# A two-layer hybrid block on one core: the late weights' low parts in one subtraction for two halves, and the SSD norm's sums of squares on VectorE in place of POOL

## The chip, the core and the metric

The kernel runs on one core of one Trainium2 chip. The metric is device time in microseconds (us), the median of several executions. Engines: TensorE (PE; its weight loads are PEld), VectorE (DVE), ScalarE (ACT), GpSimd (POOL) and SyncE (SP), which issues the DMAs.

## The reference, cut to what matters

256 tokens of width 1024 pass through two layers (SwiGLU feed-forward, a mixer, a second feed-forward) and then through a third block with attention, a short convolution and a feed-forward. The change lies in the mixers of the two layers. A mixer projects the normed x with `w_in` and hands the result to three mixers side by side: SSD, mLSTM and RWKV-7.

```python
for l in range(DEPTH):                                        # 2 layers
    x = x + FFN_HALF * swiglu(rms_norm(x, ffn1_norm[l]), ffn1_w_gate_up[l], ffn1_w_down[l])
    u = rms_norm(x, mix_norm[l]) @ w_in[l]
    u_ssd, u_ml, u_rw = jnp.split(u, [D_SSD_IN, D_SSD_IN + D_MLSTM_IN], axis=-1)
    ...
    y = jnp.concatenate([y_ssd, y_ml, y_rw], axis=-1)
    x = x + y @ w_out[l]
    x = x + FFN_HALF * swiglu(rms_norm(x, ffn2_norm[l]), ffn2_w_gate_up[l], ffn2_w_down[l])

# the end of ssd_mixer: gate, then a norm over each of two groups of 512 channels
y = y.reshape(bsz, t, SSD_WIDTH) * jax.nn.silu(z.astype(jnp.float32))
return group_rms_norm(y, norm_g, G).astype(u.dtype)
```

## The kernel before, in words

**Split products.** Every matrix product is made of three: a weight W is split into a high part (ScalarE copies it into a tile of type fp32r) and a low part (VectorE subtracts the high part from W), and x likewise. The product is high W times high x, high W times low x and low W times high x.

**The projection.** `w_in` gives 40 tiles of 128 channels. The first 14 take weights in blocks of 128x2048 through WH and WL. The other 26, tiles 14 to 39, take the late weights. These come as 52 units of 128x512 (four k of one tile each) in the ring of weight slots, u = 0 to 51, tile 14 + u/2. For each unit ScalarE writes the high part into one of four places in the ring's third slot (`act_late_high`, L1089), VectorE subtracts in place in the first or second slot (`dve_late_low`, L1095), and TensorE does twelve matmuls (`pe_proj`, L1140 to L1142) of 256 columns. ScalarE may write high u once half u - 4 is done. The DMA of unit u + 8 waits for half u.

**What sets the order.** A mixer's work is written as strands: the projection, the scan, the RWKV and SSD strands and others, each a generator on each engine. One table of turns, the same on all engines, says in which order strands advance. Each engine executes its instructions in that order and waits on semaphores. The projection has 86 turns, two for each of i = 0 to 42. `late_at(step, ahead)` tells which unit is due at a turn: u = step + ahead - 28, for u of 4 and more. ScalarE has ahead = 3 and VectorE ahead = 2, so ScalarE makes high u + 1 in the turn in which VectorE makes low u. TensorE does half u two turns after VectorE's. In a turn i ScalarE also takes tile i from PSUM (L1191, L1192) and makes the tanh of tile i - 2 (L1181); VectorE does three taps of a convolution for tile i - 1 (L1222) and a product for tile i - 3 (L1262).

**Other strands beside it.** In the first third of a mixer ScalarE has, for RWKV, the gates (L1646), keys (L1649, L1650, L1653) and L1658, and for mLSTM the copies of q and k (L1396, L1397). VectorE has an inverse root (`dve_rsqrt`, L535 to L551) of the key norms, whose sums TensorE makes at L1609, its spreading (L1689), and the key products (L1694, L1696).

**The SSD norm.** VectorE gates Y (L2254), ScalarE squares it for each of two groups into XE, 128x1024 (L2191), POOL folds that to 128x512 and to 128x256 (L2279, L2281), TensorE sums over channels (L2148), VectorE takes the inverse root (`dve_rsqrt`) and scales (L2263). At the same time the last steps of the RWKV recurrence (L1992, L1999, L2002 on VectorE, L1773 and L1782 on TensorE, L1906 on ScalarE) and another norm's inverse root run.

Of the kernel before, what the change touches and what calls it, by code (L numbers as in the profile page):

```python
# [7 lines left out]
F32 = mybir.dt.float32  # L8
I32 = mybir.dt.int32
F32R = mybir.dt.float32r  # L10
ALU = mybir.AluOpType
# [251 lines left out]
def hybrid_kernel(nc, xin, wst, lp, sp2, cst, out):  # L263
    ctx = ExitStack()
    with ctx:
# [805 lines left out]
        def late_weights(of, l, u):  # L1071
            return of[:, late_slot(l, u % 8 // 4), 512 * (u % 4):512 * (u % 4) + 512]

        def late_high(l, u):
            return ringr[:, late_slot(l, 2), 512 * (u % 4):512 * (u % 4) + 512]

        def late_at(step, ahead):

            u = step + ahead - 4 * EARLY
            if u < 4:  # L1080
                return u // 2 + 3 if u in (-6, -4, -2, 0) else None
            return u if u < 52 else None

        def act_late_high(e, l, u):
            if u is None:
                return
            e.wait_ge(*(p_pe.on("half", l, u - 4) if u >= 4 else freed(place["w_in", l, ("two", EARLY - 1)])))
            e.wait_ge(s_late[u % 8], 16 * (u // 8 + 1 + (l * (7 if u % 8 < 4 else 6))))
            e.do.activation(late_high(l, u), late_weights(ring, l, u), ACT.Copy).then_inc(*w_act.up("late high", l, u))  # L1089

        def dve_late_low(e, l, u):
            if u is None:
                return
            e.wait_ge(*w_act.on("late high", l, u))
            e.do.tensor_tensor(late_weights(ringr, l, u), late_weights(ring, l, u), late_high(l, u).bitcast(F32), ALU.subtract).then_inc(  # L1095
                *w_dve.up("late low", l, u))

        def act_x_high(e, l, k):
# [10 lines left out]
        def pe_proj(e, l):  # L1109
            f = 2 * l  # L1110
            for i in range(43):
                n, s, b = i // 2, i % 2, tile_bank(i)
                for half in range(2):
# [11 lines left out]
                    if i < 40:  # L1125
                        for kt in range(4 * half, 4 * half + 4):
# [4 lines left out]
                                m = three(e, b[:, 0:T], turn_of("w_in", l, ("two", n)), at, XNH[:, kt, 0:T], XNL[:, kt, 0:T], kt == 0, kt == KT - 1)  # L1131
                            else:
                                u = 2 * (i - 2 * EARLY) + half
                                e.wait_ge(*w_dve.on("late low", l, u))
                                if i == 2 * EARLY:
                                    e.wait_ge(*p_act.on("xh", l, kt))
                                    e.wait_ge(*p_dve.on("xl", l, kt))
# [105 lines left out]

        def dve_proj(e, l):
            for i in range(43):
                dve_late_low(e, l, late_at(2 * i, 2))
                yield
                if split_at(i):
                    dve_low(e, turn_of("w_in", l, ("two", i // 2)) + AHEAD)
# [25 lines left out]
                if i == 13:  # L1275
                    dve_x_low(e, l, 6)
                    dve_x_low(e, l, 7)
                dve_late_low(e, l, late_at(2 * i + 1, 2))
                yield


# [801 lines left out]
        def pe_ssd(e, l):  # L2083
# [59 lines left out]
            for _ in range(3):  # L2143
                yield
            for g in range(2):
                e.wait_ge(*d_pool.on("squares", l, g))
                for c in range(2):
                    m = e.do.matmul(b[:, 2 * g + c:2 * g + c + 1], (xd, xe)[g][:, 128 * c:128 * c + 128], ones[:, 0:1], start=True, stop=True)  # L2148
            m.then_inc(*d_pe.up("sums", l))
# [51 lines left out]
        def dve_ssd(e, l):  # L2201
# [50 lines left out]
            for g in range(2):  # L2252
                yo = Y[:, 4 * g:4 * g + 4, :]
                e.do.tensor_tensor(yo, yo, XC[:, 4 * g:4 * g + 4, :], ALU.mult).then_inc(*d_dve.up("gated", l, g))  # L2254
            for _ in range(4):
                yield
            e.wait_ge(*d_pe.on("sums", l))
            dve_rsqrt(e, d_dve, b[:, 0:4], 4, 1.0 / 512, EPS, 128, ("rstd", l))
            yield
# [13 lines left out]
        def pool_ssd(e, l):  # L2273
            for _ in range(25):
                yield
            for g in range(2):
                q = (xd, xe)[g]
                e.wait_ge(*d_act.on("sq", l, g))
                e.do.tensor_tensor(q[:, 0:512], q[:, 0:512], q[:, 512:1024], ALU.add).then_inc(*d_pool.up())  # L2279
                e.wait_ge(*d_pool.last())  # L2280
                e.do.tensor_tensor(q[:, 0:256], q[:, 0:256], q[:, 256:512], ALU.add).then_inc(*d_pool.up("squares", l, g))  # L2281
            for _ in range(9):
                yield
            for k in (0, 2, 4, 6):
                pool_y_low(e, d_act, d_pool, l, k)
            yield
# [881 lines left out]
```

## Time and profile before

| | |
|---|---|
| median of 3 runs | 1691.65 us (1691.17 to 1695.12) |
| the profiled execution, its own time | 1693.02 us |
| its span | 1691.2 us |
| TensorE busy | 1644.3 us, 97% |
| VectorE busy | 1352.4 us, 80% |
| ScalarE busy | 982.1 us, 58% |
| POOL busy | 400.5 us, 24% |
| weights read from HBM | 279.53 MB |

All times inside the trace count from the start of the span. Layer 0's mixer ends at about 455 us; the late weights are used in layer 0 from 249 to 411 us and in layer 1 until 1078. The busy time of an instruction includes the end in which the next one has already begun, so the chain of waits shows a little less for each of a row of instructions than the list of instructions does. The number in brackets behind a row is the time for which the engine stood idle before it, and who ended the wait.

### The profile page before, as it was taken

To read this page: it belongs to the slowest core of one execution; us is meant where nothing else is said; L and a number is where in the kernel's file an instruction comes from. 1 tells how busy PE (TensorE), PEld (TensorE's weight loads), DVE (VectorE), ACT (ScalarE), POOL (GpSimd) and SP (SyncE) were. 2 spreads that over 40 slices of the span, in tenths; PEclk is the share of its full clock that TensorE was granted. 3 is DMA by queue.
4 is the path that set the end of the run, shared out by engine and by line. 5 is a ranking of instruction groups with operands and counts; after the bars stand their busy time and mean duration, and the time that the engine had idled before them with its cause. 6 is when DMAs were issued, how large, how long until landed. Compare 5 with 4: busy or idle time off the path is not lost.

```text
span 1691.2 us, 34343 instructions
## 1 busy us (share of the span) xinstructions
PE 1644.3 (97%) x14376; PEld 1503.0 (89%) x14376; DVE 1352.4 (80%) x2263; ACT 982.1 (58%) x1787; POOL 400.5 (24%) x312
## 2 busy tenths in 40 slices
PE   9999999998999999999999999899999999999997
PEld 7888998898898888888898989799888898999987
DVE  6887789999768886788778999876887675889974
ACT  5775448635457764676445764455774556457652
POOL 1673000000115740377100000011763100211110
PEclk9999999999899999999999999899999999999999
DMA  7765634312266655576462431135675632345442
GB/s 262 258 258 197 220 102 121 107 40 78 78 241 233 242 195 207 215 256 226 172 226 76 125 107 47 53 127 203 235 263 171 226 140 101 111 162 188 163 161 100
DMA packets 96233, 282.78 MB, mean 167 GB/s; under 512 B 7376, under 2 KB 61264, under 8 KB 73040
## 3 DMA queue, kind: packets, MB, share of 16 engines
q1 hardware_dynamic: 96080, 280.60, 47.2%
q8 instruction: 113, 1.85, 0.4%
q14 instruction: 40, 0.33, 0.1%
HBM read 279.53 MB, written 1.05 MB: 166 GB/s over the span
## 4 chain that ended last, share of the span: by engine, by line
PE 76%; DVE 19%; ACT 3%; issue 1%; DMA 1%; POOL 0%; SPq 0%; DVEq 0%; ACTq 0%
PE banks L528 29%; PE banks L529 15%; PE banks L520 8%; PE banks L521 7%; PE banks L522 7%; DVE ringr L1095 3%; DVE XC L1222 1%; DVE WL L491 1%; PE banks L1773 1%; PE banks L573 1%; DVE MS L2231 1%; PE banks L1782 1%; DVE ML L1535 1%; DMA ring<-wst 1%; PE banks L1140 1%
## 5 line engine op out<-in xcount | busy, mean ns | idle before, releaser
L491 DVE TENSOR_TENSOR WL<-ring,WH 128x2048 fp32r<-128x2048 f32 (+1 forms) x218 | 457.4, 2110 | 108.8 <-ACT WH L486 108.6
L528 PE MATMUL banks<-XNP,WH 128*128 128x512 f32 x1408 | 496.5, 397 | 3.4 <-DVE XNP L627 2.4
L486 ACT ACTIVATE WH<-ring 128x2048 fp32r<-128x2048 f32 (+1 forms) x222 | 378.9, 1715 | 52.2 <-PE banks L522 46.2
L529 PE MATMUL banks<-XNP,WL 128*128 128x256 f32 x1408 | 392.3, 279 | 0.0
L528 PEld LDWEIGHTS banks<-XNP,WH 128*128 128x128 f32 x1408 | 265.0, 188 | 65.5 <-DVE XNP L627 3.2
L990 POOL TENSOR_TENSOR HP<-G,HP 128x256 fp32r<-128x256 f32 x110 | 210.3, 1912 | 311.6 <-ACT HP L802 311.6
L528 PE MATMUL banks<-HP,WH 128*128 128x512 f32 x770 | 267.7, 392 | 0.8 <-POOL HP L990 0.7
L529 PEld LDWEIGHTS banks<-XNP,WL 128*128 128x128 f32 x1408 | 265.6, 189 | 0.0
L529 PE MATMUL banks<-HP,WL 128*128 128x256 f32 x770 | 215.2, 280 | 0.0
L528 PEld LDWEIGHTS banks<-HP,WH 128*128 128x128 f32 x770 | 144.5, 188 | 33.4 <-POOL HP L990 1.6
L520 PE MATMUL banks<-XNQ,WH 128*128 128x256 f32 (+1 forms) x544 | 157.9, 290 | 2.2 <-ACT BIG L2497 1.0
L522 PE MATMUL banks<-XNQ,WL 128*128 128x256 f32 (+1 forms) x544 | 154.8, 285 | 0.0
L521 PE MATMUL banks<-XNQ,WH 128*128 128x256 f32 (+1 forms) x544 | 154.4, 284 | 0.0
L529 PEld LDWEIGHTS banks<-HP,WL 128*128 128x128 f32 x770 | 144.6, 188 | 0.0
L1141 PE MATMUL banks<-XNr,ringr 128*128 128x256 f32 x416 | 116.4, 280 | 0.0
L900 DVE TENSOR_TENSOR G<-banks,G 128x512 f32<-128x512 f32 x88 | 60.4, 686 | 67.9 <-ACT G L896 67.6
L2279 POOL TENSOR_TENSOR XE<-XE 128x512 f32<-128x512 f32 x4 | 5.1, 1269 | 443.2 <-ACT XE L2191 443.1
L520 PEld LDWEIGHTS banks<-XNQ,WH 128*128 128x128 f32 x544 | 103.9, 191 | 6.7 <-issue 3.9
L521 PEld LDWEIGHTS banks<-XNQ,WH 128*128 128x128 f32 x544 | 104.3, 192 | 0.0
L522 PEld LDWEIGHTS banks<-XNQ,WL 128*128 128x128 f32 x544 | 104.1, 191 | 0.0
L790 POOL TENSOR_TENSOR ring<-ring 128x512 f32<-128x512 f32 x72 | 96.6, 1341 | 28.2 <-ACT ring L782 24.5
L589 POOL TENSOR_TENSOR ACC<-ACC,SQ 128x256 f32<-128x256 f32 x48 | 35.6, 741 | 260.8 <-ACT SQ L863 200.4
(538 smaller groups left out, 3786.5 us busy)
## 6 DMA issues: line engine op xcount, KB each, us to landing
ring<-wst SPq DMA_DIRECT2D x179, 1024.0 KB, 4.8
ring<-wst SPq DMA_DIRECT2D x80, 704.0 KB, 4.2
ring<-wst SPq DMA_DIRECT2D x104, 256.0 KB, 2.8
LP<-lp SPq DMA_DIRECT2D x1, 1872.0 KB, 8.4
LP<-lp SPq DMA_DIRECT2D x4, 448.0 KB, 5.5
ring<-wst SPq DMA_DIRECT2D x2, 512.0 KB, 6.1
X<-xin SPq DMA_DIRECT2D x2, 512.0 KB, 7.0
out<-X SPq DMA_DIRECT2D x4, 256.0 KB, 2.2
```

The lines of the kernel that those rows point to most:

```text
L486: e.do.activation(WH[:, slot[q], 0:n], ring[:, slot_at(i), 0:n], ACT.Copy).then_inc(*w_act.up("high", q))
L491: e.do.tensor_tensor(WL[:, slot[q], 0:n], ring[:, slot_at(i), 0:n], WH[:, slot[q], 0:n].bitcast(F32), ALU.subtract).then_inc(*w_dve.up("lo ...
L520: e.do.matmul(o, WH[:, s, cols], xh, start=first, stop=False)
L521: e.do.matmul(o, WH[:, s, cols], xl, start=False, stop=False)
L522: return e.do.matmul(o, WL[:, s, cols], xh, start=False, stop=last)
L528: e.do.matmul(b[:, :], WH[:, s, cols], x.rearrange("p s t -> p (s t)"), start=first, stop=False)
L529: return e.do.matmul(b[:, 0:T], WL[:, s, cols], x[:, 0, :], start=False, stop=last)
L790: e.do.tensor_tensor(wt[:, 0:512], wt[:, 0:512], wt[:, 512 * p:512 * p + 512], ALU.add).then_inc(*f_pool.up())
L900: e.do.tensor_tensor(G2[:, j % 3, :, :], pair_halves(j, 0), G2[:, j % 3, :, :], ALU.add).then_inc(*f_dve.up("added", f, j))
L990: e.do.tensor_tensor(HL[:, j, :], HT[:, j % 3, :], HH[:, j, :].bitcast(F32), ALU.subtract).then_inc(*f_pool.up("hl", f, j))
L1095: e.do.tensor_tensor(late_weights(ringr, l, u), late_weights(ring, l, u), late_high(l, u).bitcast(F32), ALU.subtract).then_inc(*w_dve.up(" ...
L1141: e.do.matmul(b[:, 0:T], wh, XNr[:, kt, :], start=False, stop=False)
```

## The change

VectorE makes the low parts of two units in one subtraction of 128x1024. `late_pair_at` gives the pair's even unit: pair 0 and pair 2 stand where low 1 and low 3 stood, every other pair u where low u stood; where low u + 1 stood for odd u + 1 there is nothing. The pair waits for high u + 1, and TensorE waits, for both halves, on the pair. ScalarE's, TensorE's and SyncE's instructions and their order are the same as before. In the SSD strand the two folding additions of each group go from POOL to VectorE, the first group's one turn after the gating, the second's a turn later. The number of turns of each strand stays.

```diff
+        def late_pair_at(step):
+
+            u = late_at(step, 2)
+            return u - 1 if u in (1, 3) else u if u is not None and u >= 4 else None
+
...
+        def late_tile(of, l, u):
+            return of[:, late_slot(l, u % 8 // 4), 512 * (u % 4):512 * (u % 4) + 1024]
+
         def dve_late_low(e, l, u):
-            if u is None:
+
+            if u is None or u % 2:
                 return
-            e.wait_ge(*w_act.on("late high", l, u))
-            e.do.tensor_tensor(late_weights(ringr, l, u), late_weights(ring, l, u), late_high(l, u).bitcast(F32), ALU.subtract).then_inc(
+            e.wait_ge(*w_act.on("late high", l, u + 1))
+            high = ringr[:, late_slot(l, 2), 512 * (u % 4):512 * (u % 4) + 1024]
+            e.do.tensor_tensor(late_tile(ringr, l, u), late_tile(ring, l, u), high.bitcast(F32), ALU.subtract).then_inc(
                 *w_dve.up("late low", l, u))
...
-                                e.wait_ge(*w_dve.on("late low", l, u))
+                                e.wait_ge(*w_dve.on("late low", l, u - half))
...
-                dve_late_low(e, l, late_at(2 * i, 2))
+                dve_late_low(e, l, late_pair_at(2 * i))
...
-                dve_late_low(e, l, late_at(2 * i + 1, 2))
+                dve_late_low(e, l, late_pair_at(2 * i + 1))
...
-                e.wait_ge(*d_pool.on("squares", l, g))
+                e.wait_ge(*d_dve.on("squares", l, g))
...
-            for _ in range(4):
-                yield
+            yield
+            for g in range(2):
+                q = (xd, xe)[g]
+                e.wait_ge(*d_act.on("sq", l, g))
+                e.do.tensor_tensor(q[:, 0:512], q[:, 0:512], q[:, 512:1024], ALU.add).then_inc(*d_dve.up())
+                e.wait_ge(*d_dve.last())
+                e.do.tensor_tensor(q[:, 0:256], q[:, 0:256], q[:, 256:512], ALU.add).then_inc(*d_dve.up("squares", l, g))
+                yield
+            yield
...
-            for g in range(2):
-                q = (xd, xe)[g]
-                e.wait_ge(*d_act.on("sq", l, g))
-                e.do.tensor_tensor(q[:, 0:512], q[:, 0:512], q[:, 512:1024], ALU.add).then_inc(*d_pool.up())
-                e.wait_ge(*d_pool.last())
-                e.do.tensor_tensor(q[:, 0:256], q[:, 0:256], q[:, 256:512], ALU.add).then_inc(*d_pool.up("squares", l, g))
```

What stands in VectorE's row in the first third of layer 0's mixer, from the spreading of the key norms (L1689, in the changed kernel L1699; lines below L1081 move by 5 to 10) to tile 22. Before, the first low is low 16, then come 17 and 18:

```order
L1689 COPY RV<-SM 128x1024 [waits r_dve]
L1095 TENSOR_TENSOR ringr<-ring,ringr 128x512 [waits w_act]
L1262 SCALAR_TENSOR_TENSOR BC<-G,BC 128x256 [waits p_act]
L1222 SCALAR_TENSOR_TENSOR XC<-XP,LP,XC 128x256 [waits p_act]
L1222 SCALAR_TENSOR_TENSOR XC<-XP,LP,XC 128x256 [waits p_dve] x2
L1095 TENSOR_TENSOR ringr<-ring,ringr 128x512 [waits w_act] x2
L1262 SCALAR_TENSOR_TENSOR BC<-G,BC 128x256 [waits p_act]
```

And now, with pair 16 and pair 18:

```order
L1699 COPY RV<-SM 128x1024 [waits r_dve]
L1105 TENSOR_TENSOR ringr<-ring,ringr 128x1024 [waits w_act]
L1272 SCALAR_TENSOR_TENSOR BC<-G,BC 128x256 [waits p_act]
L1232 SCALAR_TENSOR_TENSOR XC<-XP,LP,XC 128x256 [waits p_act]
L1232 SCALAR_TENSOR_TENSOR XC<-XP,LP,XC 128x256 [waits p_dve] x2
L1105 TENSOR_TENSOR ringr<-ring,ringr 128x1024 [waits w_act]
L1272 SCALAR_TENSOR_TENSOR BC<-G,BC 128x256 [waits p_act]
```

The pair stands in the place of low 16, with both units' work and high 17's semaphore; low 17, behind the convolution, is gone.

VectorE's row at the tail of layer 0's mixer, from the end of one inverse root (L551) to the beginning of the SSD norm's. Before:

```order
L551 SCALAR_TENSOR_TENSOR SM<-SM 128x8 [waits s_dve]
L2002 SCALAR_TENSOR_TENSOR YV<-banks,KP,RV 128x64 [waits l_dve2,l_pe2]
L2002 SCALAR_TENSOR_TENSOR YV<-banks,KP,RW 128x64 [waits l_dve3,l_pe3]
L2002 SCALAR_TENSOR_TENSOR YV<-banks,KP,RV 128x64 [waits l_dve0,l_pe0]
L2002 SCALAR_TENSOR_TENSOR YV<-banks,KP,RV 128x64 [waits l_dve1,l_pe1]
L497 TENSOR_TENSOR WL<-ring,WH 128x1024 [waits w_act]
L1992 TENSOR_SCALAR RV<-YV,KP 128x64 [waits l_dve2]
```

And now:

```order
L551 SCALAR_TENSOR_TENSOR SM<-SM 128x8 [waits s_dve]
L2269 TENSOR_TENSOR XE<-XE 128x512 [waits d_act]
L2271 TENSOR_TENSOR XE<-XE 128x256 [waits d_dve]
L2012 SCALAR_TENSOR_TENSOR YV<-banks,KP,RV 128x64 [waits l_dve2,l_pe2]
L2012 SCALAR_TENSOR_TENSOR YV<-banks,KP,RW 128x64 [waits l_dve3,l_pe3]
L2012 SCALAR_TENSOR_TENSOR YV<-banks,KP,RV 128x64 [waits l_dve0,l_pe0]
L2012 SCALAR_TENSOR_TENSOR YV<-banks,KP,RV 128x64 [waits l_dve1,l_pe1]
L497 TENSOR_TENSOR WL<-ring,WH 128x1024 [waits w_act]
L2269 TENSOR_TENSOR XE<-XE 128x512 [waits d_act]
L2271 TENSOR_TENSOR XE<-XE 128x256 [waits d_dve]
L2002 TENSOR_SCALAR RV<-YV,KP 128x64 [waits l_dve2]
```

The first group's additions stand ahead of the four products with PSUM (L2002 before, L2012 now), the second group's behind them and behind a subtraction for `w_out`.

## Rows read from the trace of the kernel before

**Rows 1.** The page: TensorE's busy time, and the chain's shares by engine.

```profile
PE 1644.3 (97%) x14376; PEld 1503.0 (89%) x14376; DVE 1352.4 (80%) x2263; ACT 982.1 (58%) x1787; POOL 400.5 (24%) x312
...
PE 76%; DVE 19%; ACT 3%; issue 1%; DMA 1%; POOL 0%; SPq 0%; DVEq 0%; ACTq 0%
```

**Rows 2.** Windows: stretch, its length, busy times of PE, PEld, DVE, ACT, POOL, PEclk, DMA.

```profile
262.00:300.00 38.00, 37.10 (x297) 35.74 (x296) 36.06 (x88) 31.01 (x74) 0.00 (x0) 1.00 0.45 131
425.00:427.00 2.00, 1.94 (x40) 1.93 (x40) 2.00 (x7) 0.34 (x2) 0.00 (x0) 0.50 0.01 4
```

**Rows 3.** The chain of waits, layer 0: start, us on the chain, what.

```profile
286.56 0.35 DVE BIG L1694
...
389.50 0.60 DVE ringr L1095
```

**Rows 4.** Lines L1095 and L497: duration min/median/max in ns, first and last start.

```profile
L1095 DVE TENSOR_TENSOR ringr<-ring,ringr x104: 620/683/694, 240.4 to 1062.1; 128x512 fp32r<-128x512 f32 x104
...
L497 DVE TENSOR_TENSOR WL<-ring,WH x8: 1210/1217/1220, 425.3 to 1123.0; 128x1024 fp32r<-128x1024 f32 x8
```

**Rows 5.** Timeline of ScalarE, layer 0's first third: start, us, line, tile, [idle before].

```profile
262.90 1.18 ACT L1089 ACTIVATE ringr<-ring 128x512 fp32r<-128x512 f32 x2
...
267.57 1.70 ACT L1649 ACTIVATE RV<-BIG,LP 128x256 f32<-128x256 f32 x4
...
270.22 1.14 ACT L1089 ACTIVATE ringr<-ring 128x512 fp32r<-128x512 f32 x2
...
278.68 2.51 ACT L1658 ACTIVATE RV<-LATE,KP,LP 128x256 f32<-128x256 f32 x4
281.10 1.14 ACT L1089 ACTIVATE ringr<-ring 128x512 fp32r<-128x512 f32 x2
...
286.43 0.63 ACT L1089 ACTIVATE ringr<-ring 128x512 fp32r<-128x512 f32 x1
```

**Rows 6.** Timeline of VectorE, there and in layer 1, and of TensorE's L1140.

```profile
261.34 0.67 DVE L1095 TENSOR_TENSOR ringr<-ring,ringr 128x512 fp32r<-128x512 f32 x1
...
270.86 1.29 DVE L1095 TENSOR_TENSOR ringr<-ring,ringr 128x512 fp32r<-128x512 f32 x2 [0.58 <-ACT ringr L1089]
...
279.93 0.69 DVE L1095 TENSOR_TENSOR ringr<-ring,ringr 128x512 fp32r<-128x512 f32 x1
...
938.76 1.29 DVE L1095 TENSOR_TENSOR ringr<-ring,ringr 128x512 fp32r<-128x512 f32 x2 [0.57 <-ACT ringr L1089]
...
269.48 0.28 PE L1140 MATMUL banks<-G2r,ringr 128*128 128x256 f32 x1
...
269.84 0.28 PE L1140 MATMUL banks<-G2r,ringr 128*128 128x256 f32 x1
...
280.76 0.35 PE L1140 MATMUL banks<-G2r,ringr 128*128 128x256 f32 x1
```

**Rows 7.** Timeline of the mixers' tails: VectorE, POOL and TensorE in layer 0, TensorE in layer 1.

```profile
419.25 1.34 DVE L1992 TENSOR_SCALAR RW<-GAP,KP 128x64 f32<-128x64 f32 x1
...
420.67 0.75 DVE L1992 TENSOR_SCALAR RV<-GAP,KP 128x64 f32<-128x64 f32 x1
...
421.53 1.22 DVE L537 TENSOR_SCALAR SM<-SM 128x8 int32<-128x8 int32 x1
422.78 0.17 DVE L539 TENSOR_TENSOR SM<-SM 128x8 f32<-128x8 f32 x1
422.98 0.58 DVE L541 SCALAR_TENSOR_TENSOR SM<-SM 128x8 f32<-128x8 f32 x1
...
424.49 0.28 DVE L2002 SCALAR_TENSOR_TENSOR YV<-banks,KP,RV 128x64 f32<-128x64 f32 x1
...
419.27 1.27 POOL L2279 TENSOR_TENSOR XE<-XE 128x512 f32<-128x512 f32 x1 [221.84 <-ACT XE L2191]
...
425.06 0.48 PE L1782 MATMUL banks<-BIG,GAP 64*64 64x64 f32 x4 [3.34 <-DVE YV L2002]
...
1092.68 0.48 PE L1782 MATMUL banks<-BIG,GAP 64*64 64x64 f32 x4 [2.12 <-DVE YV L2002]
```

## The prediction

> **Names.** The late weights of one layer are 52 units u of 128x512 (tile i = 14 + u/2, first half for even u). "High u" is ScalarE's copy at L1089, "low u" VectorE's subtraction at L1095, "half u" the twelve matmuls of L1140 to L1142 that use them, "pair u" the new 128x1024 subtraction of u and u+1.
>
> **What bounds the kernel now.** I read the page's busy line and the engine shares of the chain first. TensorE is busy for 97% of the span, and VectorE is on the chain for 19% of it [rows 1]. So most of the program is matmuls that this change leaves alone, and the mixers have to be read by stretch. In the mixer's first third VectorE is busy for 36.06 of 38.00 us, TensorE for 37.10, ScalarE for 31.01 [rows 2]: three engines in lockstep, none with room. The chain of waits says which one sets the pace. It enters VectorE at lows 11 and 12, for which VectorE waits 0.58 us until 270.86 [rows 6], and it is there at the key product (L1694) at 286.56 and at low 50 at 389.50 [rows 3]. Time added to VectorE there is added to the kernel. In the mixer's tail TensorE stands idle for 3.34 us until VectorE delivers L2002 at 424.49 [rows 7].
>
> **Part 1, the instruction itself.** Lows on the chain take 0.60 us each when one follows another (two last 1.29 us [rows 6], one alone 0.68 [rows 4], so a follower starts 0.61 behind, and by the chain 0.60 [rows 3]); a 128x1024 subtraction takes 1.22 [rows 4], and with the same overlap of 0.08 us gives way after 1.14. A pair thus saves 1.20 - 1.14 = 0.06 us, and 52 of them 3.1 us. The Trainium skill would lead one to expect more: "VectorE: DVE Perf Modes", section "The DRAIN you can't avoid", gives 266 ns as the part of an instruction outside its drain and advises fewer operations; if a merge saved all of it, 52 merges would save an estimated 13.8 us. The rows here leave 0.06 us for each, and no number below uses that page.
>
> In fact even less of it is on the chain. Behind L1694 the chain has 20 lows (21 to 40), and later 46 to 50, one of which stands in [rows 3]. It loses 25 x 0.60 = 15.0 us and gets the pairs 22 to 40 and 46 to 50, 13 x 1.14 = 14.8. That is 0.2 us per layer.
>
> **Part 1, the new wait.** Pair u stands where low u stood, but it waits for high u+1. ScalarE's order is unchanged, and its high u+1 comes in the same turn of the projection, behind whatever ScalarE has to do for the other mixers. Low u could use high u, made a turn before. Where ScalarE runs late, VectorE now waits in front of it, with the convolutions' L1222 behind it in its queue, and TensorE gets half u later. I follow this through layer 0:
>
> 1. Pair 6 stands at the slot of low 6, 261.34 [rows 6]. High 7 starts at 262.90, the first of two in 1.18 us [rows 5], and takes 0.63, so the pair runs from 263.55 to 264.7. Half 10 starts at 269.48, its second k at 269.84 [rows 6]; four such steps are 1.42 us, so TensorE is at half 6 at 263.8, and it now waits 0.9 us.
> 2. ScalarE takes tile 17 (halves 6 and 7) from PSUM, and then has 2.65 us of key work from 267.57 until the highs 11 and 12 at 270.22 [rows 5]. All that comes 0.9 later: high 11 ends at 271.76. VectorE, with L1222 and pair 8 done, is at pair 10 at 269.6 and waits 2.2 us, until 271.8; the pair ends at 272.95. Half 10 moves from 269.48 to 272.95, 3.5 us later.
> 3. Now halves 10 to 13 run without a stop, with L1609's norms between; half 13 ends at about 280.3. ScalarE takes that tile and does the four L1658 (2.51 us) before the highs 17 and 18, which moves them from 281.10 [rows 5] to 283.6. Pair 16 stands at low 16's slot (279.93 before [rows 6]); VectorE is there at 282.9, waits for high 17 until 284.3 and is free at 285.35. Low 16 set it free at 280.53: it is 4.8 us late. Half 16 moves from 280.76 to 285.45.
> 4. High 21 (286.43 before [rows 5]) stands behind the copies of q and k, which wait for matmuls behind half 17, now over at 289.3. It ends at about 291.4. VectorE has waited since 290.0, pair 20 ends at 292.6, and L1694, at 286.56 on the chain before [rows 3], starts 6.1 us late.
>
> From there the chain is VectorE's, and what follows has its slots far enough behind ScalarE. So I carry 6.1 us per layer. Layer 1 has the same order and the same first wait (0.57 us at 938.76 [rows 6] against 0.58): 12.2 us for both. The bounds: nothing, if these waits were absorbed, and some 7 us per layer, if pairs 28 and 48, whose highs end within 0.3 us of their slots, add theirs.
>
> **Part 2, the sums of squares.** Before, POOL's four additions start at 419.27, and four of VectorE's instructions beside them take 1.34, 0.75, 1.22 and 0.58 us for 64 or 8 columns [rows 7]; the first ends at 420.59, POOL's first addition at 420.54. Undisturbed, such small ones take 0.17 (L539) to 0.28 (L2002) [rows 7]. So POOL's work costs VectorE about 1.1 + 0.5 + 1.05 + 0.4 = 3.05 us per layer, just ahead of L2002, on which TensorE waits. The change takes this away and puts the first group's two additions into the same place: 0.68 for 128x512 [rows 4], 0.4 for 128x256 (L1694 gives way after 0.35 [rows 3]), together 1.1 us with nothing to overlap them. The second group comes behind L2002, ahead of a wait of VectorE for TensorE of over 1 us; it is hidden, and costs 1.1 if that cover goes. L2002 comes 3.05 - 1.1 = 1.95 us earlier in layer 0. In layer 1 TensorE's idle time is 2.12 us [rows 7] and its preceding matmuls then end last: 1.5 us. Sum 3.5 us. The bounds are 1.9 (0.8 and 1.1 lost to the order of the queue) and 6, if the clock holds (below). The Trainium skill ("GPSIMD Engine Reference", section "Key points") says that GpSimd contends with VectorE's two-input and 2-port instructions; the ends above agree with it, and by it the additions would have no such victims on VectorE.
>
> **Sum.** The profiled execution took 1693.02 us with a span of 1691.2, the median is 1691.65; I add the differences to the median. 1691.65 + 12.2 - 0.4 - 3.5 = 1700.0 us.
>
> **Rivals.**
> - Faster: the waits are absorbed. If high u+1 is done before pair u's slot, VectorE doesn't wait, and what is left is 1691.65 - 3.1 - 3.5 = 1685.1. The deciding point is high 7 against 261.34 and high 11 against VectorE's arrival. For it: VectorE now waits for a high for only 0.58 us in this stretch. Against it: high 11 starts at 270.22, later than the slot, and ScalarE's order doesn't change. 10%. The skill's advice on fewer instructions points here.
> - Half: pairs 10 and 20 wait, but ScalarE catches up at the keys (its L1658 needn't be late by the whole 2.5 us): 3 us per layer, 1691.65 + 6 - 3.5 = 1694.2. 20%.
> - The clock: TensorE gets stops of about 2.2 us at halves 10 and 16. The granted clock is 1.00 in this stretch and 0.50 after the idle 3.34 us of the tail, 1.2 of 2.4 GHz [rows 2, 7]. If it falls here too for some 3 to 5 us in either layer, matmuls take twice as long: 1700.0 + 4 to 8 = 1704 to 1708. 13%.
> - The tail's shorter stop keeps the clock up there: 1700.0 - 2.5 = 1697.5. 7%.
>
> **How the numbers follow.** The forecast has 50%, and with 10, 20, 13 and 7 that is all. The range reaches from 1690.0 (the half case with the tail at its better bound) to 1707.0 (the clock's case but for its end); outside lie the faster rival and a part of the clock's. About 0.3%, or 5.1 us, is what a measurement can tell from no change: 1686.6 to 1696.7. Faster 0.10, same 0.20, slower 0.70.
>
> **What would show it.** Right: VectorE waits for L1089 at pairs 6, 10, 16 and 20, over 6 us per layer together, TensorE waits for the lows at halves 10 and 16 for about 2.2 us, and L1694 starts near 292.6. L1992 and L537 take no more than 0.28 and 0.17, and TensorE's stop before L1782 is near 1.4 us. Wrong: VectorE's idle time in the first third stays below 2 us (then the faster rival), or L1694 is 3 us late (the half case), or a clock of 0.50 in the first third.

## The result and the profile after

| | before | changed |
|---|---|---|
| median of 5 runs | 1694.53 us (1691.17 to 1697.4) | 1704.29 us (1701.97 to 1704.99) |
| ratio | | 1.0057, 95% interval 1.004 to 1.0073 |
| the profiled execution, its own time | 1693.02 us | 1701.97 us |
| its span | 1691.2 us | 1700.2 us |

The changed kernel is slower. The page shows where the chain went. Beside [rows 1], VectorE has 44 instructions fewer and POOL 8, and VectorE's share of the chain falls from 19% to 15% while ScalarE's rises from 3% to 5%:

```profile
PE 1642.8 (97%) x14376; PEld 1499.9 (88%) x14376; DVE 1348.3 (79%) x2219; ACT 983.0 (58%) x1787; POOL 391.7 (23%) x304
...
PE 77%; DVE 15%; ACT 5%; issue 1%; DMA 1%; POOL 0%; SPq 0%; DVEq 0%; ACTq 0%
```

**First third of layer 0.** The same windows as in [rows 2], and two stretches behind it (columns as there):

```profile
262.00:300.00 38.00, 31.79 (x230) 30.58 (x231) 28.36 (x60) 24.71 (x56) 0.00 (x0) 0.91 0.39 114
...
271.00:275.00 4.00, 4.00 (x22) 4.00 (x23) 3.86 (x8) 1.55 (x4) 0.00 (x0) 0.60 0.15 43
285.00:288.00 3.00, 2.63 (x12) 2.54 (x12) 2.93 (x6) 1.03 (x3) 0.00 (x0) 0.58 0.11 32
```

VectorE is busy for 28.36 us where it was for 36.06, TensorE for 31.79 where it was for 37.10, and the clock has fallen. VectorE's timeline gives the pairs 6, 10, 14, 16 and 20 and the key product behind them (L1704, before L1694; in brackets the idle time ahead):

```profile
261.08 1.23 DVE L1105 TENSOR_TENSOR ringr<-ring,ringr 128x1024 fp32r<-128x1024 f32 x1 [2.17 <-ACT ringr L1094]
...
269.58 1.23 DVE L1105 TENSOR_TENSOR ringr<-ring,ringr 128x1024 fp32r<-128x1024 f32 x1 [2.29 <-ACT ringr L1094]
...
276.99 1.23 DVE L1105 TENSOR_TENSOR ringr<-ring,ringr 128x1024 fp32r<-128x1024 f32 x1 [1.51 <-ACT ringr L1094]
...
284.00 1.22 DVE L1105 TENSOR_TENSOR ringr<-ring,ringr 128x1024 fp32r<-128x1024 f32 x1 [1.52 <-ACT ringr L1094]
...
293.17 1.23 DVE L1105 TENSOR_TENSOR ringr<-ring,ringr 128x1024 fp32r<-128x1024 f32 x1 [3.26 <-ACT ringr L1094]
294.31 0.42 DVE L1704 TENSOR_TENSOR BIG<-BIG,RV 128x256 f32<-128x256 f32 x1
```

L1704 is at 294.31 where L1694 was at 286.56 [rows 3], though this execution was 2.0 us ahead at 253.8. TensorE's timeline shows halves 6, 10 and 16 behind pairs 6, 10 and 16, and half 32 in layer 0 and 1:

```profile
262.45 0.36 PE L1150 MATMUL banks<-G2r,ringr 128*128 128x256 f32 x1 [0.99 <-DVE ringr L1105]
...
270.95 0.36 PE L1150 MATMUL banks<-G2r,ringr 128*128 128x256 f32 x1 [2.21 <-DVE ringr L1105]
...
285.37 0.46 PE L1150 MATMUL banks<-G2r,ringr 128*128 128x256 f32 x1 [2.37 <-DVE ringr L1105]
...
328.35 0.36 PE L1150 MATMUL banks<-G2r,ringr 128*128 128x256 f32 x1 [2.01 <-DVE ringr L1105]
...
1000.32 0.36 PE L1150 MATMUL banks<-G2r,ringr 128*128 128x256 f32 x1 [2.01 <-DVE ringr L1105]
```

The waits of the stretch 255 to 300 (engine, line, what it waited for: us in total, times, longest) close the loop: VectorE for ScalarE, TensorE for VectorE, ScalarE for TensorE. In the trace of before the first was 0.6 us, once. (L1094 is ScalarE's high, L1105 VectorE's pair, L1150 and L1152 are TensorE's half.)

```profile
DVE ringr L1105 <- ACT ringr L1094: 10.7, 5, 3.3
PE banks L1150 <- DVE ringr L1105: 5.6, 3, 2.4
...
ACT ringr L1094 <- PE banks L1152: 2.6, 2, 1.6
```

**The same third in layer 1.** Here the clock stays at 1.00 (columns as above), and of the pairs 14, 16 and 20 in VectorE's timeline pair 14 has no wait:

```profile
927.00:967.00 40.00, 33.95 (x261) 31.15 (x261) 31.14 (x67) 31.98 (x76) 0.00 (x0) 1.00 0.38 108
...
950.37 1.23 DVE L1105 TENSOR_TENSOR ringr<-ring,ringr 128x1024 fp32r<-128x1024 f32 x1
...
957.44 1.23 DVE L1105 TENSOR_TENSOR ringr<-ring,ringr 128x1024 fp32r<-128x1024 f32 x1 [1.58 <-ACT ringr L1094]
...
965.15 1.23 DVE L1105 TENSOR_TENSOR ringr<-ring,ringr 128x1024 fp32r<-128x1024 f32 x1 [1.80 <-ACT ringr L1094]
966.29 0.42 DVE L1704 TENSOR_TENSOR BIG<-BIG,RV 128x256 f32<-128x256 f32 x1
```

**The tail of layer 0.** What VectorE's timeline has in the place of [rows 7]; L2002 is now L2012:

```profile
429.15 0.17 DVE L537 TENSOR_SCALAR SM<-SM 128x8 int32<-128x8 int32 x1
...
430.64 0.68 DVE L2269 TENSOR_TENSOR XE<-XE 128x512 f32<-128x512 f32 x1
431.36 0.42 DVE L2271 TENSOR_TENSOR XE<-XE 128x256 f32<-128x256 f32 x1
431.70 0.28 DVE L2012 SCALAR_TENSOR_TENSOR YV<-banks,KP,RV 128x64 f32<-128x64 f32 x1
```

L537 takes 0.17 us where it took 1.22, and no wait of TensorE for YV is left in this tail, where there was one of 3.34.

### The profile page after: what moved, and what is told of

Its sections match the earlier page's. It is cut to its first block, busy times and chain, and to the rows that moved or that the text cites. A ratio compares the mean times of both kernels' runs of the same rounds, so it can differ in the third digit from the quotient of the medians.

```text
span 1700.2 us, 34291 instructions
## 1 busy us (share of the span) xinstructions
PE 1642.8 (97%) x14376; PEld 1499.9 (88%) x14376; DVE 1348.3 (79%) x2219; ACT 983.0 (58%) x1787; POOL 391.7 (23%) x304
## 4 chain that ended last, share of the span: by engine, by line
PE 77%; DVE 15%; ACT 5%; issue 1%; DMA 1%; POOL 0%; SPq 0%; DVEq 0%; ACTq 0%
PE banks L528 29%; PE banks L529 15%; PE banks L520 8%; PE banks L522 7%; PE banks L521 7%; DVE ringr L1105 2%; PE banks L1783 1%; DVE WL L491 1%; PE banks L1150 1%; PE banks L1152 1%; PE banks L1151 1%; PE banks L573 1%; DVE XC L1232 1%; PE banks L1792 1%; ACT ringr L1094 1%
```

## How the experiments are read

**Landmarks.** Four of VectorE's instructions cut each mixer in three: KP out of LP (253.8 us before, 922.2 in layer 1), the key product (286.5, 954.4), the SSD gating (416.8, 1084.5) and a product into YV (442.4, 1109.2). The drift of a landmark is its start less its start in the trace of before. A part's loss is the difference of two drifts, so what an execution lost or gained elsewhere drops out. Starts are read to 0.1 us, so an entry can be off by 0.1. The table gives it for layer 0 / layer 1, and TensorE's time at half clock (granted 0.50) in the first third, summed from windows of 1 us.

| kernel | first third | half clock there | middle | tail |
|---|---|---|---|---|
| changed | +9.8 / +6.8 | 6.8 / 0 | +1.4 / +2.1 | -3.4 / -2.5 |
| e1_pairs_only | +13.2 / +6.8 | 17.1 / 0 | +2.1 / +1.2 | +0.4 / +0.9 |
| e2_tail_only | 0 / 0 | 0 / 0 | +0.6 / +0.1 | -3.6 / -1.0 |
| e3_pairs_late_tail | 0 / 0 | 0 / 0 | +2.4 / +2.0 | -1.7 / -4.1 |
| e4_pairs_early | +9.8 / +6.8 | 6.8 / 0 | -0.3 / -0.5 | +0.4 / +0.3 |
| e5_two_at_slot | +6.8 / +8.3 | 3.4 / 6.8 | +2.2 / +2.1 | -0.8 / +1.3 |
| e6_pe_waits_pair | +5.2 / +4.3 | 6.8 / 5.4 | +16.9 / +14.5 | -0.8 / +0.9 |
| e7_no_folds | +3.1 / 0 | 6.8 / 0 | +1.4 / 0 | -6.0 / -5.2 |
| e9_highs_early_pairs | -0.2 / +0.3 | 0 / 0 | +0.8 / +0.3 | -1.9 / -2.5 |
| e12_changed_again | +11.3 / +11.3 | 10.2 / 10.2 | +2.2 / +2.2 | -5.0 / -4.1 |

In the middle the kernels without pairs are not all at 0 either: e2, e7, e10 and e11 drift by 0.6 to 1.4 us in layer 0, e8 by 1.8 in layer 1. Up to 359 us (1027 in layer 1) they stand at 0.0; the drift comes in a step before 377 (1043). In e7, e8, e10 and e11 TensorE stands idle there for 0.9 to 1.5 us with nothing in the trace that releases it, as here in e7:

```profile
369.48 0.33 PE L1782 MATMUL banks<-RV 64*64 64x64 f32 x3 [1.49 <-issue]
```

So what a middle loses behind 359 us need not be an effect of the pairs, up to some 1.5 us.

**Equal clock.** Every execution comes with its mean granted clock. The kernel before ran 65 times beside the experiments, on three chips: mean 1693.1 us at a mean clock of 0.9849. A straight line through them falls by 1385 us per unit of clock and accounts for 66% of the variance. One us at half clock lowers the mean by 0.5/1693 = 0.0003, so it costs 0.41 us by this line. The last column is a kernel's mean less the line at that kernel's mean clock, with its standard error. It is a correlation, and it is extrapolated a little for e1 and e6. It also takes out whatever the change itself does to the clock. The kernel before lies 0.9 us above the line in the comparison with e1, e2, e3 and e5 and 0.3 below it in the other two, so values from different comparisons can differ by another us.

| kernel | runs | mean clock | mean us | at equal clock |
|---|---|---|---|---|
| changed | 5 | 0.9876 | 1703.7 | +14.4 +- 0.9 |
| e12_changed_again | 6 | 0.9852 | 1706.6 | +13.9 +- 0.8 |
| e1_pairs_only | 4 | 0.9802 | 1716.3 | +16.8 +- 1.1 |
| e4_pairs_early | 4 | 0.9828 | 1710.2 | +14.2 +- 1.0 |
| e5_two_at_slot | 4 | 0.9832 | 1710.6 | +15.2 +- 0.9 |
| e6_pe_waits_pair | 4 | 0.9788 | 1730.4 | +28.8 +- 1.2 |
| e3_pairs_late_tail | 12 | 0.9868 | 1690.9 | +0.5 +- 0.6 |
| e2_tail_only | 7 | 0.9891 | 1685.6 | -1.6 +- 0.9 |
| e11_tail_again | 12 | 0.9888 | 1686.1 | -1.6 +- 0.7 |
| e8_tail_later | 12 | 0.9865 | 1691.5 | +0.6 +- 0.6 |
| e7_no_folds | 5 | 0.9890 | 1683.2 | -4.2 +- 1.0 |
| e9_highs_early_pairs | 12 | 0.9875 | 1688.8 | -0.7 +- 0.6 |
| e10_highs_early_single | 12 | 0.9892 | 1687.1 | -0.1 +- 0.8 |

## The two parts apart

**e1_pairs_only** is the changed kernel with the additions back on POOL.

```diff
-            e.wait_ge(*w_act.on("late high", l, u))
+            e.wait_ge(*w_act.on("late high", l, u + 1))
...
-                                e.wait_ge(*w_dve.on("late low", l, u))
+                                e.wait_ge(*w_dve.on("late low", l, u - half))
```

> The pairs alone, the additions left on POOL. Theory (VectorE waits for ScalarE's high u + 1): the changed kernel is 9.7 us slower as a whole and its tails gained 3.4 and 2.5 us in its profile, so this one is 13 to 16 us slower than before. Rival (the tails gained nothing that lasts, their gain is given back behind them): 9 to 11 us slower.

Measured: 1716.55 us against 1694.28, ratio 1.0131 (1.0107 to 1.0155). That is 22.3 us slower, beyond the 13 to 16 that I expected; at equal clock it is 16.8. Part 1 alone is worse than both parts together, and the waits of layer 0's first third are longer where the clock fell longer:

```profile
DVE ringr L1105 <- ACT ringr L1094: 14.1, 5, 4.8
```

In layer 1 no half clock fell into this third, and the loss is 6.8 us, the same as in the changed kernel.

**e2_tail_only** is the kernel before with the additions on VectorE; **e11_tail_again** is the same in a later comparison.

```diff
-            for _ in range(4):
-                yield
+            yield
+            for g in range(2):
...
+                e.do.tensor_tensor(q[:, 0:512], q[:, 0:512], q[:, 512:1024], ALU.add).then_inc(*d_dve.up())
```

> The additions on VectorE alone, the low parts as before. Theory: L1992 and the inverse root run undisturbed, TensorE's stop before L1782 shrinks from 3.3 to about 1.3 us, 3.5 to 6 us faster than before. Rival (gain given back behind the tail, where VectorE has 1.1 us more): within 1 us of before.

> The additions on VectorE alone, once more, because its interval of 0.9927 to 0.9973 was wide. Theory: 4 to 7 us faster than before by the median, 6 us of it in the two tails. Rival (the first measurement had short tails by the clock's chance): 2 us or less.

Measured: 1686.3 us against 1694.28, ratio 0.995 (0.9927 to 0.9973), and 1685.9 against 1691.39, ratio 0.996 (0.9942 to 0.9978). This half is a gain, and this kernel beats both. Its tail in VectorE's and TensorE's timeline, to be held against [rows 7]:

```profile
419.57 0.25 DVE L1992 TENSOR_SCALAR RW<-GAP,KP 128x64 f32<-128x64 f32 x1
...
420.25 0.17 DVE L537 TENSOR_SCALAR SM<-SM 128x8 int32<-128x8 int32 x1
...
422.81 0.28 DVE L2002 SCALAR_TENSOR_TENSOR YV<-banks,KP,RV 128x64 f32<-128x64 f32 x1
...
423.38 0.33 PE L1782 MATMUL banks<-BIG,GAP 64*64 64x64 f32 x4 [1.34 <-DVE YV L2002]
```

The gating starts at 417.14 here and at 416.82 before, L2002 at 422.81 and 424.49: 5.67 us behind it and not 7.67. So 2.0 us are gained up to L2002, and TensorE's stop is 1.34 us. The medians gain 8.0 us (3.5 to 6 were expected) and 5.5 us (4 to 7 expected), and at equal clock 1.6. The rest goes with the clock: its mean is 0.989 in both comparisons, and 0.985 for the kernel before. As both comparisons show it, it belongs to the change; by what step the change raises it, no run isolates.

## Which pairs, and is it the length or the place

**e3_pairs_late_tail** has pairs for u under 4 and from 22 on, single subtractions for 4 to 21, and the additions on VectorE.

```diff
+            if u is None or u % 2 and in_pair(u):
...
+        def in_pair(u):
+            u -= u % 2
+            return u < 4 or u >= 22
```

> Pairs only for units 0 to 3 and 22 to 51, units 4 to 21 one by one as before; additions on VectorE. Theory (the loss sits in the waits for highs 7 to 21): VectorE waits for no high before unit 22, what is left of the loss are the 1.4 and 2.1 us that the changed kernel lost between 305 and 412 us of a layer's mixer, so with the tails' gain 0 to 3 us faster than before. Rival (the pair as such is slow wherever it stands, by its length or by TensorE's later start): the loss shrinks only in proportion, 16 of 25 pairs' worth, and this kernel is over 4 us slower than before.

Measured: 1691.95 us against 1694.28, ratio 0.9979 (0.9965 to 0.9994). It is 2.3 us faster, where 0 to 3 were expected. The first third loses nothing. The middle, which the prediction took to be free, loses 2.4 and 2.0 us. Pairs 28, 42 and 48 wait there. VectorE's timeline has pair 28, TensorE's half 32:

```profile
307.82 1.23 DVE L1114 TENSOR_TENSOR ringr<-ring,ringr 128x1024 fp32r<-128x1024 f32 x1 [0.59 <-ACT ringr L1098]
...
321.29 0.36 PE L1159 MATMUL banks<-G2r,ringr 128*128 128x256 f32 x1 [2.01 <-DVE ringr L1114]
```

In the trace of before TensorE stands idle for 1.41 us ahead of half 32, which starts at 320.26; here it waits 0.6 us longer, since pair 32, behind a long row of VectorE's work, ends 0.6 us after low 32's place. Up to 332 us the drift is 0.4 to 1.0 in either layer; another 1.5 comes before 377; pair 42 waits 0.30 us at 347.21 and pair 48 0.33 at 377.20. Which of the moved instructions costs how much of that I haven't taken apart. At 350 us (1018 in layer 1) the drift is 1.7 and 1.2, where no kernel without pairs has any; 0.6 of it is given back by 359, and what comes behind lies where those kernels, too, have their step. Against e2_tail_only the whole is +2.1 us at equal clock, with an error of about 1.

**e4_pairs_early** has pairs only for u under 22, and POOL's additions.

```diff
+        def in_pair(u):
+            u -= u % 2
+            return u < 22
```

> The counterpart of the kernel with pairs from unit 22 on: pairs only for units 0 to 21, from 22 on one by one, additions on POOL. Theory (the waits for highs 7 to 21 are the loss): from the mixer's first scaling to L1694 each layer loses 6.1 to 6.8 us without a fall of the clock, more with one, and between L1694 and the gating of Y nothing: 12 to 18 us slower than before. Rival (the loss is spread over all pairs): 5 to 8 us slower, and the middle of the mixer loses 1.5 to 2 us here too.

Measured: 1710.6 us against 1692.79, ratio 1.0104 (1.008 to 1.0128). It is 17.8 us slower, where 12 to 18 were expected. The whole loss is in the first third, 6.8 us in layer 1 and 9.8 in layer 0 with 6.8 us at half clock, and the middle gains 0.3 to 0.5.

**e5_two_at_slot** has two subtractions of 128x512 at the pair's place, behind the wait for high u + 1; TensorE waits for its own low as before, and POOL adds.

```diff
+            e.wait_ge(*w_act.on("late high", l, u + 1))
+            for v in (u, u + 1):
+                e.do.tensor_tensor(late_weights(ringr, l, v), late_weights(ring, l, v), late_high(l, v).bitcast(F32), ALU.subtract).then_inc(
+                    *w_dve.up("late low", l, v))
```

> At the place of pair u stand the wait for high u + 1 and then two subtractions of 128x512, low u and low u + 1, and TensorE waits for each half's own; additions on POOL. It differs from the pairs-only kernel in the length of the instruction alone. Theory (the wait costs, the length nothing): the same waits for highs, and 12 to 18 us slower than before, within 3 us of the pairs-only kernel. Rival (the length and TensorE's wait for both halves cost): within 3 us of before.

Measured: 1710.82 us against 1694.28, ratio 1.0097 (1.0076 to 1.0118). No instruction is longer than before, and nearly the whole loss is there. At equal clock it is 1.6 us less than e1_pairs_only, about the size of the error. With 0.41 us for each us at half clock, the first third loses 6.8 - 1.4 = 5.4 and 8.4 - 2.8 = 5.6 us, an estimate, against 6.8 with the pair. So it is the wait for high u + 1 that costs most, and the pair's length together with TensorE's wait for both of its halves accounts for up to 1.4 us per layer.

**e6_pe_waits_pair** is the kernel before, except that TensorE waits for low u + 1 ahead of both halves.

```diff
-                                e.wait_ge(*w_dve.on("late low", l, u))
+                                e.wait_ge(*w_dve.on("late low", l, u - half + 1))
```

> VectorE's and ScalarE's instructions, places and waits are those of before; TensorE alone waits, for both halves, on low u + 1. This is TensorE's part of the change without VectorE's. Theory (VectorE's wait in front of its own queue is what costs most): here half u waits only until low u + 1 of before, which ended 0.5, 1.3 and 2.1 us after half u began at u = 6, 8 and 10; but this wait delays ScalarE's highs in turn, so 2 to 5 us per layer, 4 to 10 us slower than before, clearly less than the pairs. Rival (the loss is TensorE's wait for two units at once): as slow as the pairs, 14 us and more.

Measured: 1730.87 us against 1692.79, ratio 1.0223 (1.02 to 1.0247), the worst of all, and far beyond the 4 to 10 us that I expected. By its number it is the rival (14 us and more). The first third loses 5.2 and 4.3 us, with 6.8 and 5.4 us at half clock; the middle 16.9 and 14.5. TensorE's timeline and the waits of the stretch 290 to 420:

```profile
329.59 0.36 PE L1140 MATMUL banks<-G2r,ringr 128*128 128x256 f32 x1 [2.96 <-DVE ringr L1095]
...
PE banks L1140 <- DVE ringr L1095: 13.3, 7, 3.5
```

Before, low 33 stands at 321.90 and low 32 at 319.43: a turn of the projection lies between the two, and in the middle other strands' work fills it. TensorE now starts half 32 on the later one. So this kernel doesn't isolate TensorE's wait as I had meant: its cost lies mostly in the middle, where the changed kernel, whose pair stands at low u's place, has little. It shows that one wait on the later of two operands costs whatever stands between them. It suggests, without showing it, that the early place of the pair was the right one of the two.

## The cause undone

**e9_highs_early_pairs** is the changed kernel, with ScalarE making high u + 1 directly behind high u, a turn ahead of where it was. **e10_highs_early_single** is e2_tail_only with the same edit.

```diff
-                act_late_high(e, l, late_at(2 * i, 3))
+                if 2 * i + 3 - 4 * EARLY < 5:
+                    act_late_high(e, l, late_at(2 * i, 3))
                 yield
-                act_late_high(e, l, late_at(2 * i + 1, 3))
+                u = late_at(2 * i + 1, 3)
+                act_late_high(e, l, u)
+                if u is not None and u >= 4:
+                    act_late_high(e, l, u + 1)
```

> The changed kernel, with one order moved: ScalarE makes high u + 1 of a pair (u of 4 and more) directly behind high u, so one turn earlier, ahead of the copies of its tile and of the other mixers' work. Theory (the pair waits for ScalarE's place in the row, not for ScalarE's or TensorE's work): VectorE's waits for highs in the first third fall from 9 to 11 us in a layer's profile to under 2, TensorE's for low parts with them, and the kernel is 3 to 8 us faster than before, 13 us and more faster than the changed one. Rival (high u + 1 needs half u - 3, and ScalarE now waits for TensorE instead and holds up its own row): the changed kernel's loss stays by half or more, 0 us or more slower than before.

> The same order of the highs with the low parts one by one and the additions on VectorE: the control for the kernel before it. Theory: low parts one by one had next to no waits for highs, so it gains nothing by it and is within 3 us of the kernel with the additions alone; beside the pairs with early highs it is 1 to 3 us slower (52 times 0.06 us). Rival (early highs cost ScalarE waits for TensorE): 4 us and more slower than the additions alone.

Measured: 1688.62 us and 1687.0 against 1691.39, ratios 0.9981 (0.9966 to 0.9995) and 0.9968 (0.9955 to 0.9981); the changed kernel has 1.0085 (1.0065 to 1.0105) in the same comparison. So early highs make it 18.8 us faster (13 and more were expected), and 2.8 us faster than before, just short of the expected 3 to 8. Pairs 10, 12 and 20 in VectorE's timeline of e9, and a row of the waits of its whole execution:

```profile
268.06 1.22 DVE L1105 TENSOR_TENSOR ringr<-ring,ringr 128x1024 fp32r<-128x1024 f32 x1
...
272.13 1.23 DVE L1105 TENSOR_TENSOR ringr<-ring,ringr 128x1024 fp32r<-128x1024 f32 x1 [1.08 <-ACT ringr L1094]
...
286.73 1.23 DVE L1105 TENSOR_TENSOR ringr<-ring,ringr 128x1024 fp32r<-128x1024 f32 x1 [0.20 <-ACT ringr L1094]
...
ACT ringr L1094 <- PE banks L1152: 17.5, 29, 1.2
```

VectorE's waits for highs are 2.6 us in all, where the changed kernel has 21.3. The first third loses nothing. ScalarE now waits for TensorE 29 times, since a high may be written only once half u - 4 is done, but it has the time. That settles the cause in the first third: not the pair, but its wait for a high that ScalarE makes in the same turn. The two kernels differ by 0.6 us at equal clock, with an error of about 1, where 1 to 3 were expected for the pairs: the pairs themselves gain nothing that can be measured here. Nor does either kernel beat e11_tail_again, with single low parts and late highs (1685.9 us in the same comparison).

**e12_changed_again** is the changed kernel in this comparison; one line of its change:

```diff
+            e.wait_ge(*w_act.on("late high", l, u + 1))
```

> The changed kernel once more, beside the others on one chip. Theory: 8 to 14 us slower than before; in each layer VectorE waits again 2.1 to 2.3 us at pairs 6 and 10, 1.5 at pair 16 and 1.5 to 3.3 at pair 20, while the us at half clock in the first third differ from run to run between 0 and some 10. Rival (the 5 runs of the first measurement were unlucky in the clock): under 5 us.

Measured: 1707.42 us (1701.09 to 1710.11), 16.0 us slower than before, where 8 to 14 were expected; at equal clock it is 13.9. Pair 20 waits 4.8 us in either layer, beyond the expected 3.3. Its profiled execution has 56.1 us at half clock in all, that of the first result 35.7, and is 4.9 us longer in span.

## POOL's part in the tail

**e7_no_folds** leaves POOL's four additions per layer out; POOL writes one column in place of each group's two, so that the sums of squares are incomplete.

```diff
-                e.do.tensor_tensor(q[:, 0:512], q[:, 0:512], q[:, 512:1024], ALU.add).then_inc(*d_pool.up())
-                e.wait_ge(*d_pool.last())
-                e.do.tensor_tensor(q[:, 0:256], q[:, 0:256], q[:, 256:512], ALU.add).then_inc(*d_pool.up("squares", l, g))
+                e.do.memset(SM[:, 188 + g + 2 * l:189 + g + 2 * l], 0.5).then_inc(*d_pool.up("squares", l, g))
```

> POOL leaves the four folding additions of each layer out and only signals, with a write of one column; so the SSD norm's sums of squares are incomplete. All else is as before. Theory (POOL's additions hold up VectorE's small instructions): L1992, L537 and L541 take 0.25, 0.17 and 0.17 us, L2002 starts about 3.0 us earlier against the gating of Y in layer 0, and the kernel is 5 to 9 us faster than before, 1 to 3 us faster than with the additions on VectorE. Rival (those instructions are slow for their own reasons, a dependency or a late operand): they stay at 1.34, 1.22 and 0.58 us and the kernel is within 1 us of before.

Measured: 1683.43 us against 1692.79, ratio 0.9943 (0.9923 to 0.9964). VectorE's timeline:

```profile
421.80 0.25 DVE L1992 TENSOR_SCALAR RW<-GAP,KP 128x64 f32<-128x64 f32 x1
...
422.49 0.17 DVE L537 TENSOR_SCALAR SM<-SM 128x8 int32<-128x8 int32 x1
...
424.42 0.28 DVE L2002 SCALAR_TENSOR_TENSOR YV<-banks,KP,RV 128x64 f32<-128x64 f32 x1 [0.35 <-PE banks L1782]
```

L1992 and L537 take 0.25 and 0.17 us with nothing else changed on VectorE, where they took 1.34 and 1.22 [rows 7]: it was POOL's work that held them up. The whole is 9.4 us faster, a little beyond the expected 5 to 9, and 4.2 at equal clock. L2002 comes 5.04 us behind the gating (419.38), 2.6 less than before, and there it waits for TensorE: the last 0.4 of the 3.05 us were not to be had.

**e8_tail_later** is e2_tail_only with both groups' additions one turn later.

```diff
+            yield
+            yield
+            for g in range(2):
```

> As the additions on VectorE alone, but each group's one turn later: the first behind L2002 and a subtraction for w_out, the second behind L1992. Theory (the first group's 1.1 us in front of L2002 stand on the path): TensorE's L1782 comes 1.1 us earlier per layer, but its sums L2148 then wait for the second group, about 1.5 us behind where they could start, so 0 to 2 us slower than with the additions in the place of the change, still 3 us or more faster than before. Rival (the sums' wait is hidden by other matmuls): 1 to 2 us faster than the change's place.

Measured: 1691.12 us against 1692.79, ratio 0.9991 (0.9978 to 1.0004). It is 1.7 us faster than before, where 3 or more were expected. L2002 comes early, as in e7_no_folds, but TensorE's timeline has a new stop ahead of the sums of each group:

```profile
425.24 0.61 PE L2148 MATMUL banks<-C,XE 128*128 128x1 f32 x4 [0.96 <-DVE XE L2262]
426.95 0.61 PE L2148 MATMUL banks<-C,XE 128*128 128x1 f32 x4 [1.11 <-DVE XE L2262]
```

I had expected a wait of about 1.5 us for the second group only. TensorE waits for both groups, and 2.1 us of stops in layer 0 and 2.3 in layer 1 give the gain back. The order of the change, additions ahead of L2002, is the better one.

## Why the prediction was right, and where it was off

The forecast was 1700.0 us in a range of 1690.0 to 1707.0, slower with 0.70. The time is 1704.29, inside the range and slower. The steps:

1. **The new wait: right.** The replay said that pairs 6, 10, 16 and 20 wait, over 6 us together. They do, with 2.17, 2.29, 1.52 and 3.26 us. TensorE's stops at halves 6, 10 and 16 were put at 0.9, 2.2 and about 2.2, and are 0.99, 2.21 and 2.37. With the 2.0 us that this execution was ahead, half 10 starts at 270.95 + 2.0 = 272.95, where the replay had it.
2. **Pair 14: right where the clock holds.** I let halves 10 to 13 run without a stop and gave pair 14 no wait. In layer 0 it waits 1.51 us, and from there all is later than in the replay: half 16 at 285.37 + 2.0 = 287.4 and not 285.45. But in layer 0 the clock is at 0.50 from 271.8 to 275.2, in just these halves. In layer 1, at 1.00, pair 14 has no wait, and L1704 starts 39.0 us behind the landmark at KP, where the replay has 292.66 - 253.79 = 38.9. In e1_pairs_only, e4_pairs_early and e12_changed_again, too, pair 14 waits (1.1 to 1.5 us) where the clock has fallen behind half 10, and not where it hasn't. So the replay of the waits was right within some 0.2 us in layer 1, and what it mainly lacked in layer 0 was the clock.
3. **The size: 6.8 us per layer, not 6.1,** where the clock holds; layer 1 of three kernels gives it (changed, e1, e4). Most of the difference there is that I carried layer 0's sum over to layer 1: the kernel before needs 32.7 us from KP to the key product in layer 0, and 32.1 in layer 1. Each us at half clock adds about 0.4: (9.8 - 6.8)/6.8 = 0.44 in the changed kernel, (13.2 - 6.8)/17.1 = 0.37 in e1_pairs_only, 3.1/6.8 = 0.46 in e7_no_folds, which loses nothing else there.
4. **The instruction itself: wrong in sign.** The 0.2 us per layer behind L1694 were a gain in the sum, and I let what follows have its slots far enough behind ScalarE. The middle lost 1.4 and 2.1 us; pairs 28 and 48, which stood in my bounds, did wait. How much of it is the pairs' is less sure: by 359 us (1027 in layer 1) it is 0.5 and 0, and behind that a stop of TensorE of 1.1 us (1047.8 in layer 1) has no releaser in the trace. At equal clock the late pairs cost 2.1 us (e3 less e2), with an error of about 1. The Trainium skill's advice on fewer instructions ("VectorE: DVE Perf Modes", section "Rules for kernel authors") finds no support in this case: 52 merges brought nothing that could be measured between e9 and e10.
5. **The tail: right at its first step, too high in the sum.** L2002 was to come 1.95 us earlier in layer 0 and comes 2.0 earlier in e2_tail_only. At equal clock the whole kernel gets 1.6 us and not 3.5, with an error of 0.7 to 0.9. The landmarks give 4.6 for both tails, some 1.4 of it clock (3.4 us less at half clock in the two mixers together). Another 0.6 goes in layer 0's middle. Where the rest is given back, the traces don't tell me.
6. **The clock in the first third (13%)** came true beside the forecast, in one layer or both. The five kernels with the front waits have it in 7 of 10 layers, behind halves 10 and 16 mostly. Of the seven without them (before, e2, e3, e8, e9, e10, e11) none has it in 14 layers. Not all of it is theirs, though: e7_no_folds and e6_pe_waits_pair have 6.8 us from 254 to 261 in layer 0, ahead of any such wait, and e1_pairs_only has as much at the same place. By the prediction's own signs "a clock of 0.50 in the first third" counts against the forecast case, and for this rival.
7. **The tail's clock stays up (7%)** was the rival that I priced and weighed too low. I gave it 2.5 us and 7%. In e2 and e11 it is the larger part of the gain: (0.989 - 0.985) x 1385 = 5.5 us. The profiled executions agree in direction. From 5 us ahead of the gating to 40 behind it, both layers together, the half clock is 27.3 us before, 34.1 in the four other kernels with POOL's additions (e1, e4, e5, e6), 23.9 in e2 and e11, 13.7 in both profiles of the changed kernel, and 10.2 in e7.
8. **The faster and the half rival** fell: no layer of the changed kernel lost under 6.8 us in its first third.

The sum with measured terms, at equal clock: +14.2 for the early pairs (e4), +2.1 for the late ones (e3 less e2), -1.6 for the tail: +14.7, against +14.4 and +13.9 measured. The changed kernel's mean clock of 0.9876 in the first result gives back (0.9876 - 0.9849) x 1385 = 3.7 us. From the 65 runs' mean of 1693.1 that is 1693.1 + 14.7 - 3.7 = 1704.1; the five runs have a mean of 1703.7. Against that my 1700.0 had 4.5 us too little for part 1 (11.8 for 14.2 + 2.1), 1.9 too much gain in the tail and a starting value 1.4 lower, and no term for the clock, which took 3.7 back. So the mechanism was right, and that the time lies within 4.3 us of the forecast is partly luck: three errors of one sign, 7.8 us together, met one of 3.7 of the other. The lower bound of the range has a slip too: the half case with the tail at its better bound is 1691.65 + 6 - 6 = 1691.7, not 1690.0.

## What to carry over

When two operations are merged, the merged one stands in the first one's place and waits for the second one's operand. Before merging, look at when the last operand is made against the slot, in the table of turns as well as in the trace, and move its maker ahead with it. When a small part of VectorE's work sits beside POOL's just ahead of something that TensorE waits for, look at the durations of instructions of equal shape: here one of 1.2 us among ones of 0.2 was the sign of the neighbour. And before small changes are compared, set the runs' mean clocks beside their times.

## What the runs showed of the hardware

- **POOL and VectorE.** Four of VectorE's instructions on 64 or 8 columns lasted 1.34, 0.75, 1.22 and 0.58 us beside POOL's additions of 128x512 and 128x256, and 0.17 to 0.25 without them (e7_no_folds). I had expected this; its full effect up to L2002 was 2.6 us per layer, not 3.05, since TensorE then ends last. The Trainium skill ("GPSIMD Engine Reference", section "Key points") names the contention, and these runs agree that there is one. Which kinds of VectorE's instructions meet it, they don't tell.
- **The clock sets the spread.** 65 executions of one kernel range from 1687.93 to 1700.65 us, with mean clocks from 0.980 to 0.989, and two thirds of the variance goes with the clock. Two executions of the changed kernel differed by 20.4 us of half clock and 4.9 us of span.
- **Equal stops, unequal clocks.** Half 32 waits 2.01 us in both layers of the changed kernel. In layer 0 the granted clock is 0.50 behind it, from 329 to 333 us, in layer 1 it stays at 1.00. And 3.4 us at half clock (322.7 to 326.1) behind the same stop in e3_pairs_late_tail, layer 0, hardly moved the next row of VectorE: at 332 us its drift has grown by 1.0, and by 0.4 in layer 1, which kept its clock.
